# Mean-subtracting norms by token half, with the routing constants issued from ScalarE's queue

## The reference, cut to what matters

```python
for i in range(DEPTH):                                  # DEPTH = 2
    mix = differential_attention(h, ...) if i == 0 else dsa_sparse_mla(h, ...)
    h = layer_norm(alpha * h + mix, ln_g[i, 0], ln_b[i, 0])
    h = layer_norm(alpha * h + memory_cross_attention(h, ...), ln_g[i, 1], ln_b[i, 1])
    h = layer_norm(alpha * h + hierarchical_moe(h, ...), ln_g[i, 2], ln_b[i, 2])

def layer_norm(x, g, b):
    mu = mean(x); xc = x - mu; var = mean(xc * xc)
    return xc * rsqrt(var + 1e-5) * g + b
```

## Time and profile before

| | |
|---|---|
| median of 3 runs | 1678.61 us (1677.8 to 1679.4) |
| the profiled execution | 1678.4 us, its span 1676.5 us |
| granted clock of TensorE, mean | 0.993 of full speed |
| busy, share of the span | PE 98%, PEld 74%, DVE 55%, ACT 43% |
| chain that ended last | PE 89%, DVE 6%, ACT 2%, DMA 1%, issue 1% |

### The profile page before, as it was taken

How to read it: one execution, slowest core, us unless ns; L and a number is a source line. 1 busy time by engine, 2 the same in 40 slices (tenths; PEclk the granted TensorE clock), 3 DMA queues, 4 the chain that set the end, 5 groups by cost and what they waited for, 6 DMA issues and landing times.

```text
span 1676.5 us, 28896 instructions
## 1 busy us (share of the span) xinstructions
PE 1636.4 (98%) x12140; PEld 1244.3 (74%) x12140; DVE 924.0 (55%) x1976; ACT 724.2 (43%) x1394; POOL 5.0 (0%) x6
## 2 busy tenths in 40 slices
PE   9999999999999999999999999999989999999996
PEld 8888888786798688889888986555546798655553
DVE  6677666654467467668658774212135776521213
ACT  5577555423343455556557553121124655312111
POOL 0000000000000000000000000000000000000000
PEclk9999999999999999999999999999989999999998
DMA  8613453533201455435451546999992254699995
GB/s 345 251 76 142 160 215 136 183 109 142 90 4 61 181 187 193 184 139 194 174 198 51 194 170 257 427 425 424 427 397 90 100 194 170 256 426 425 424 426 231
DMA packets 36326, 372.07 MB, mean 222 GB/s; under 512 B 7264, under 2 KB 8416, under 8 KB 11360
## 3 DMA queue, kind: packets, MB, share of 16 engines
q1 hardware_dynamic: 32928, 364.09, 54.3%
q10 hardware_dynamic: 3264, 6.07, 1.2%
HBM read 369.09 MB, written 1.05 MB: 221 GB/s over the span
## 4 chain that ended last, share of the span: by engine, by line
PE 89%; DVE 6%; ACT 2%; DMA 1%; issue 1%; DVEq 0%; SPq 0%; ACTq 0%
PE ps L660 27%; PE ps L2428 13%; PE ps L1261 10%; PE ps L2451 7%; PE ps L1262 5%; PE ps L884 3%; PE ps L2440 2%; PE ps L1005 2%; PE ps L2411 2%; PE ps L1844 2%; PE ps L1813 2%; PE ps L986 1%; PE ps L2915 1%; PE ps L2482 1%; DMA routing<-in_rank 1%; PE ps L437 1%
## 5 line engine op out<-in xcount | busy, mean ns | idle before, releaser
L1261 PE MATMUL ps<-ffn_x,ffn_w 128*128 128x512 f32 x704 | 250.0, 399 | 0.2
L2428 PE MATMUL ps<-ring,expert_inputs 128*64 128x256 f32 x1984 | 227.8, 382 | 0.0
L652 ACT CAST w_h<-ring 128x512 fp32r<-128x512 f32 x240 | 149.4, 624 | 138.1 <-PE ps L660 130.1
L655 DVE TENSOR_TENSOR w_l<-ring,w_h 128x512 fp32r<-128x512 f32 x240 | 164.0, 689 | 66.3 <-ACT w_h L652 62.4
L1262 PE MATMUL ps<-ffn_x,ffn_w 128*128 128x256 f32 x704 | 197.7, 281 | 0.0
L2428 PEld LDWEIGHTS ps<-ring,expert_inputs 128*64 128x64 f32 x1984 | 137.0, 137 | 67.0
L655 DVE TENSOR_TENSOR ffn_w<-ring,ffn_w 128x1024 fp32r<-128x1024 f32 x132 | 157.7, 1221 | 15.4 <-ACT ffn_w L652 12.9
L1261 PEld LDWEIGHTS ps<-ffn_x,ffn_w 128*128 128x128 f32 x704 | 132.3, 188 | 33.9 <-DVE ffn_x L499 0.8
L660 PE MATMUL ps<-w_h,x_h 128*128 128x512 f32 x384 | 150.1, 391 | 0.0
L660 PE MATMUL ps<-w_h,x_l 128*128 128x512 f32 x384 | 149.5, 389 | 0.0
L660 PE MATMUL ps<-w_l,x_h 128*128 128x512 f32 x384 | 149.4, 389 | 0.0
(11 more groups left out here) (381 smaller groups left out, 2677.2 us busy)
## 6 DMA issues: line engine op xcount, KB each, us to landing
ring<-in_w_moe SPq DMA_DIRECT2D x62, 2048.0 KB, 14.0
ring<-in_w_proj SPq DMA_DIRECT2D x37, 2048.0 KB, 8.0
ring<-in_w_ffn SPq DMA_DIRECT2D x22, 3072.0 KB, 10.1
ring<-in_w_moe SPq DMA_DIRECT2D x64, 1024.0 KB, 14.9
ring<-in_w_b_in SPq DMA_DIRECT2D x1, 2496.0 KB, 13.3
ring<-in_w_lora SPq DMA_DIRECT2D x1, 2048.0 KB, 7.9
rows<-in_w_moe SPq DMA_DIRECT2D x2, 1024.0 KB, 10.1
h<-in_w_moe SPq DMA_DIRECT2D x2, 1024.0 KB, 5.0
```

What stands on the lines that cost most here:

```text
L652: act.copy(high, x).then_inc(ready.up(), 1)
L655: return dve.tensor_tensor(low, x, high.bitcast(F32), ALU.subtract)
L1261: pe.matmul(bank(c), w[0][:, k, :], x_pair[:, k].rearrange("p a s -> p (a s)"), start=k == 0, stop=False, skip_group_check=True)
L2428: last = pe.matmul(bank(0)[g * SLOTS_E:(g + 1) * SLOTS_E, 0:2 * P], x[:, k, e * SLOTS_E:(e + 1) * SLOTS_E], wg[g][:, k, :], start=(k == 0) ...
```

## The change

The norm kind of the four norms becomes `halves`. In the projection ahead of it, DVE now takes the mean and variance of half 0 right after the statistics of half 0 (`half_stats`), ACT takes its root and normalises both pieces of half 0 (`half_roots`), and only then does DVE turn to the product of half 1, whose two pieces it normalises itself. PE transposes all of half 0, runs three fills, and then transposes all of half 1 (`halves_pe`); the block or blocks `k` whose bank still holds the last product are taken last within half 0. The fills behind the projection go from four to two, and the three at the head of the next block move between the two halves. In the mixture ACT, not SP, issues the three small transfers, in the order bias, rank, slots, after its new work and the scaled identity `alpha`.

```diff
+        def half_stats(dve, t):
+            s, spread, root, inverse, ready = (sig(x) for x in ("dve_step", "mean_square", "row_root", "inverse_ready", "normed_dve"))
+            dve.wait_ge(*until(s))
+            link(dve, "dve_step", dve.bn_aggr(mv[:, t, :], bn[:, t, :, :]))
+            dve.tensor_scalar(ms[:, t:t + 1], var[:, t:t + 1], LN_EPS, None, ALU.add).then_inc(spread.up(), 1)
+            dve.wait_ge(root.sem, root.at(t + 1))
+            link(dve, "dve_step", dve.reciprocal(rstd[:, t:t + 1], std[:, t:t + 1]))
+            if t == 0:
+                dve.scalar_tensor_tensor(shift[:, 0:1], mean[:, 0:1], -1.0, rstd[:, 0:1], ALU.mult, ALU.mult).then_inc(inverse.up(), 1)
+            else:
+                for c in row_halves():
+                    dve.tensor_scalar(h[:, 1, c], h[:, 1, c], mean[:, 1:2], rstd[:, 1:2], ALU.subtract, ALU.mult).then_inc(ready.up(), 1)
+
+        def half_roots(act):
+            spread, root, inverse, ready = (sig(x) for x in ("mean_square", "row_root", "inverse_ready", "normed_act"))
+            for t in range(T):
+                act.wait_ge(spread.sem, spread.at(t + 1))
+                act.activation(std[:, t:t + 1], ms[:, t:t + 1], ACT.Sqrt).then_inc(root.up(), 1)
+                if t == 0:
+                    act.wait_ge(inverse.sem, inverse.at(1))
+                    for c in row_halves():
+                        act.activation(h[:, 0, c], h[:, 0, c], ACT.Identity, bias=shift[:, 0:1], scale=rstd[:, 0:1]).then_inc(ready.up(), 1)
...
+        def halves_pe(pe, norm, place, after, late=(), free=7):
+            tp = sig("transposed")
+            for t in range(T):
+                if t:
+                    fill(pe, 3, free)
+                for k in [k for k in range(KD) if t or k not in late] + [k for k in late if t == 0]:
+                    if k % 4 == 0 or k in late:
+                        pe.wait_ge(*end["halves"][t][k // 4])
+                    if k in late and t == 0:
+                        pe.wait_ge(*end["last_product_read"])
+                    ins = pe.transpose(place(k)[:, t * P:(t + 1) * P], norm.src[:, t, k * P:(k + 1) * P], ident[:])
+                    if t and k in after:
+                        ins.then_inc(tp.up(after[k]), after[k])
...
-                        fill(pe, 1 if plain else 4)
+                        fill(pe, 1 if plain else 2)
...
                     if residual is not None and u == units - 1:
                         load_root(act)
+                        if not plain:
+                            half_roots(act)
...
                             add_residual(dve, t, u, residual, bank(T * (u % 2) + t))
+                            if u == units - 1:
+                                half_stats(dve, t)
...
-                    fill(pe, 3, end["bank"])
-                    norm_pe(pe, own_norm, turned_rows, {1: 2, 3: 2, 5: 2, 7: 2})
+                    halves_pe(pe, own_norm, turned_rows, {1: 2, 3: 2, 5: 2, 7: 2}, (6, 7))
...
                     act.activation(alpha, ident[:], ACT.Copy, scale=ALPHA).then_inc(alpha_ready.up(), 1)
-                    norm_act(act, own_norm)
+                    act.wait_ge(*end["pe"])
+                    act.dma_start(bias, d["route_b"][layer].rearrange("(o f) -> o f", o=1).broadcast_to([P, ROUTE])).then_inc(got.up(16), 16)
+                    act.dma_start(rank, d["rank"].rearrange("(o f) -> o f", o=1).broadcast_to([P, 4])).then_inc(got.up(16), 16)
+                    act.dma_start(w[:, 512:512 + 2 * P + SLOTS_E], d["slots"]).then_inc(got.up(16), 16)
...
-                    norm_dve(dve, own_norm)
...
-                    sp.wait_ge(*end["pe"])
-                    sp.dma_start(bias, d["route_b"][layer].rearrange("(o f) -> o f", o=1).broadcast_to([P, ROUTE])).then_inc(got.up(16), 16)
-                    sp.dma_start(w[:, 512:512 + 2 * P + SLOTS_E], d["slots"]).then_inc(got.up(16), 16)
-                    sp.dma_start(rank, d["rank"].rearrange("(o f) -> o f", o=1).broadcast_to([P, 4])).then_inc(got.up(16), 16)
                     last_unit = loads[j0 + EU - 1]
                     sp.wait_ge(*end["dve"])
```

More of the change, by code:

```diff
@@ L284, in add_residual @@
             link(dve, "dve_step", dve.scalar_tensor_tensor(x, x, scale, product, ALU.mult, ALU.add))
+            end["last_product_read"] = until(sig("dve_step"))
             row_stats(dve, t, c).then_inc(sig("dve_step").up(), 1)
+        def half_stats(dve, t):
[19 more added lines that the diff above has]
+                        act.activation(h[:, 0, c], h[:, 0, c], ACT.Identity, bias=shift[:, 0:1], scale=rstd[:, 0:1]).then_inc(ready.up(), 1)
         def scale_rows_by_parts(dve):
@@ L384, in norm_dve @@
         def norm_dve(dve, norm):
-            if norm.kind in ("rows", "turned"):
+            if norm.kind in ("rows", "turned", "halves"):
                 return
@@ L464, in norm_x_act @@
             tp, made, high, split = sig("transposed"), sig("x_made"), sig("x_high"), sig("x_split")
-            if norm.kind == "ln":
+            if norm.kind in ("ln", "halves"):
                 for m in ((0, 1) if k == 0 else (k + 1,)):
@@ L763, in open_rows @@
                 norm_pe(pe, norm, split_place, SPLIT_AFTER)
+            elif norm.kind == "halves":
+                halves_pe(pe, norm, split_place, SPLIT_AFTER, (1,), 0)
+                fill(pe, 2, 0)
             else:
@@ L869, in project @@
                 end.update(pe=until(tail), dve=until(sig("dve_step")), bank=7)
+                if not plain:
+                    end["halves"] = [[until(sig(x), c + 1) for c in range(2)] for x in ("normed_act", "normed_dve")]
                 if plain:
@@ L2182, in cross_attention @@
         def cross_attention(layer):
-            project_features(xT, fm(2), norm=split_norm("ln", *ln_cols(3 * layer)))
+            project_features(xT, fm(2), norm=split_norm("ln", *ln_cols(3 * layer))._replace(kind="halves"))
             o = tok(3)
@@ L2192, in mixture @@
             row_src = (d["ln_g"][3 * layer + 2], d["ln_b"][3 * layer + 2])
+            own_halves = end["halves"]
             unscaled.clear()
-            own_norm = Norm("ln", gain, shift, h, False)
+            own_norm = Norm("halves", gain, shift, h, False)
             close_part()
@@ L2511, in _ @@
                     for t in range(T):
[L2512 to L2514 removed]
+                        for normed in own_halves[t]:
+                            act.wait_ge(*normed)
                         act.copy(parts_h[0][:, t, :], h[:, t, :]).then_inc(high.up(), 1)
```

2 lines of the change are left out of this document (1 added, 1 removed).

## The result

| | before | changed |
|---|---|---|
| median of 6 runs | 1678.89 us (1677.8 to 1680.42) | 1684.97 us (1680.97 to 1688.68) |
| the profiled execution | 1678.4 us, span 1676.5 | 1680.97 us, span 1679.1 |

The ratio is 1.0032, 95% interval 1.0022 to 1.0042. So it is slower by about 0.27%, or 4.5 us, above the 0.2% named in the prediction. The median of these six runs lies 2.4 us above the range of the prediction; the two later medians, 1682.77 and 1682.48 us, lie at its upper bound of 1682.6. The profiled execution was the fastest of its six.

A forecast was written before the change was run, and what follows sets the result against it. PE was taken as the bound (89% of the chain): its stream plus its waits. Two cross attentions at -0.2 and two mixtures at 0.0 gave -0.4 us against 1678.4, so 1678.0, with the median 1678.2 us; range 1675.4 to 1682.6.

The forecast's parts named there:

- Half 0 under half 1's products: Projection: DVE ends half 0's part at about 932.8, just in time for half 1's addition at 932.92; no cost.
- Cross attention: Ahead of the first product: half 1's transposes start earlier, at 936.15, everything after unchanged; 0.2 us gained each time.
- the origin: End of the projection, from which times are counted: 932.73 ahead of the cross attention, 1001.97 in the mixture.
- The upper bound of 0.5: Cross attention: most that could be gained each time, in us, should the fills be shorter than counted.
- The mixture's logits: Mixture's front: logits ready at 1010.2 instead of 1010.67; at most 1.0 us shorter with the transfers out of the way.
- The three transfers: Mixture, moved to ACT's queue: landing taken at 1011.5, midway between early and late; no change in the mixtures.
- later issue: Mixture: ACT issues the three transfers from about 1004.2 to 1005.5, some 2 us later than before; speaks for late landing.
- upper bound, 1013.7: Mixture: latest landing, small transfers last, behind the 1 MB one; DVE reads then instead of 1011.43, losing 2.2 us.
- rival 2: Mixture, DVE's reading of the logits: constants land behind the 1 MB transfer; 2 x 2.2 - 0.4 = +4.0, 1682.6 us; chance 0.10.
- The lower bound: Mixture: earliest landing, 1009.3, from `in_inv` landing 4.2 us after its issue; earlier than the logits, gain 1.0 us.
- new idle stretches: PE's new standstills: no longer than 0.75 us, an argument against a fall of its clock.
- rivals 2 and 3: Late landing, 1682.6 us, chance 0.10; PE's clock falling in thinner filled stretches, 1683 us, chance 0.02.

The follow-up runs named there:

- the two later medians: The changed kernel itself, timed twice more beside other experiments against the kernel before: 1682.77 us, ratio 1.0026, and 1682.48 us, ratio 1.0023.
- e4: Changed kernel's norm by halves, constants loaded once some 70 us ahead, none issued in the mixture; against the kernel before: 1676.13 us, ratio 0.9977.
- e6: Changed kernel, but SP issues the 1 MB transfer only when the three constants have landed; against the kernel before: 1676.62 us, ratio 0.9985.
- e9: Kernel before with its old norm, ACT issuing the three transfers, SP's 1 MB transfer waiting for them; against the kernel before: 1677.55 us, ratio 0.9992.
- e2: Kernel before with its old norm, only the three transfers moved to ACT, behind `alpha`; against the kernel before: 1682.73 us, ratio 1.0016.

## Why the prediction was wrong

**Half 0 under half 1's products: right.** DVE was free 0.24 us ahead of half 1's addition, and the addition did not move.

**Cross attention: right mechanism, size too small,** 0.44 for 0.2 us. Half 1's first transpose was where I had it: 3.42 us behind the origin forecast, 3.46 measured. ACT's first evacuation came 3.77 behind the origin (4.03 before) and `x_l` 5.12 (5.38 before), 0.26 earlier, as the forecast of 0.24 had it. But I took the wait from `x_l` to the first product as unchanged, and wrote that two fills now end ahead of `x_l`, "so that the eight transposes taken off the path give no more". In the trace of before two fills started at 938.09, behind all sixteen transposes, and the product at 938.77 came directly behind them, 0.23 us after `x_l` was done at 938.54; now it comes 0.06 after. They did give more, 0.17 us: the fills had been the last to end. (The upper bound of 0.5 was a slip, 936.39 less 935.7 is 0.7; the 0.44 lies under both.)

**The mixture's logits: right.** Said: ready 0.5 us earlier and at most 1.0 a mixture with the transfers out of the way. Measured: 0.70, and 1.13 to 1.19 at the gather (e4) and 0.97 to 1.14 (e6).

**The three transfers: the step that failed.** "I take the middle of the two landings, 1011.5: no change in the mixtures, because what speaks for early (no queue ahead) and for late (later issue, sharing) are both in the rows and neither is nearer." The landing was 1012.67, in a kernel whose origin lay 0.54 earlier, so 1013.2 on the scale of the prediction: near its upper bound, 1013.7, and not in the middle. The place and the cause of rival 2, which I gave 0.10, were right: e6 and e9 show that the reading waits for the constants only when the 1 MB transfer is in flight beside them. The lower bound came from a transfer without traffic beside it. That case does exist here (e6: 4.4 us, against `in_inv`'s 4.2), but only with the 1 MB transfer held back, and the prediction had said itself that this transfer "no longer stands behind them". That had been a reason for late, not a reason for the middle. The later issue, which I also counted as a reason for late, was none: 1.9 us of it moved the landing by 0.1 us and less with the 1 MB transfer held back (e6 and e9), and by +0.8 and -0.4 us with it in flight (changed and e2). The price of rival 2, 2 x 2.2 us, was 1.87 + 1.32 at the readings.

**What the landing sets off: missing.** I argued that "new idle stretches are no longer than 0.75 us" and dismissed the clock with 0.02. This held only for my own landing. With a late one PE stands 2.2 to 2.6 us, and in three of six mixtures the clock falls behind it. So rivals 2 and 3 weren't wholly two cases, and I had priced them apart. The sum as the runs have it: -0.9 for the cross attentions, +3.2 for the readings, +1.1 for one fall of the clock, +3.4 us; the three ratios say 3.9 to 5.4. What is left, 0.5 to 2 us, I can't place: the profiles are single executions, and the first was the fastest of its six. The lower clock of many runs (0.9913 in the mean, 0.9930 for before) fits it in size, but where in these runs the clock fell is open.

## What to carry to other kernels

A small transfer that an engine waits for was here only as early as the large ones in flight beside it, whenever it was issued: before moving it to another queue, look at which large transfer its old place held back, and let that one wait for it. When a bound is worked out for a wait, follow it to its end: how long does PE then stand, and what did its clock do in this trace behind stretches of that length? Two rivals of which one sets off the other get one price together.

## What the runs showed of the hardware

160 KB on ACT's queue landed in 4.4 us beside the end of a ring load on SP's queue (e6), in 6.3 when issued 1.9 us sooner beside the same load (e9), and in 8.0 to 9.8 with the 1 MB transfer on SP's queue in flight as well; even 2 KB (`rank`) needed 3.9, 5.7 and 7.5 to 8.7 (medians of the two mixtures). The size of the small one mattered little, the company did: `slots` landed 0.4 to 0.5 us behind the last ring load in e6 and e9, and within 0.4 us of the 1 MB transfer, earlier or later, in e2.

PE standing still for 2.2 to 2.6 us was followed by the lower clock in three of the six mixtures of the changed kernel's profiles and not in the others (a fall behind 2.35, 2.37 and 2.60 us, none behind 2.19, 2.24 and 2.46; and none behind e2's 1.16 and 1.90). Each fall lasted 3.4 us and cost about 1.1. Over the 25 runs of this kernel, 1680.6 to 1688.7 us, the time falls by 1.3 us for each 0.001 of mean clock (correlation -0.93); over the 85 runs of before in the three groups, 1676.3 to 1681.9 us at 0.992 to 0.995, by 0.8 us (-0.53).
